# Extra TensorE products of constants in the gated-linear units of two merged mixers

## The reference, cut to what matters

```python
def hybrid_mixer(h, hc, w_in, ret_decay, gate_up, gate_b, gla_norm_g, row_pos, col_pos, need_ctx):
    lat = project_in(h, w_in)
    cx = project_in(hc, w_in)
    ...
    r_lat, r_ctx = bidirectional_scan(retention_inputs(lat, True), retention_inputs(cx, False))
    g_lat, g_ctx = bidirectional_scan(gla_inputs(lat), gla_inputs(cx))

    def merge(r, g, parts):
        ret = from_heads(head_layernorm(r)) * jax.nn.silu(parts[3])
        gla = from_heads(rmsnorm(g, gla_norm_g)) * jax.nn.silu(parts[7])
        return jnp.concatenate([ret, gla], axis=-1)

    y_lat = merge(r_lat, g_lat, lat)
    y_ctx = merge(r_ctx, g_ctx, cx) if need_ctx else None
    return y_lat, y_ctx

def bidirectional_scan(lat_in, ctx_in):
    ...
    c_f, s_f = chunked_gated_linear_attention(cq, ck, cv, ca_f, zero, False)
    x_f, _ = chunked_gated_linear_attention(q, k, v, a_f, s_f, False)
    c_b, s_b = chunked_gated_linear_attention(flip(cq), flip(ck), flip(cv), flip(ca_b), zero, True)
    x_b, _ = chunked_gated_linear_attention(flip(q), flip(k), flip(v), flip(a_b), s_b, True)
    return x_f + flip(x_b), c_f + flip(c_b)
```

## Time and profile before

| | us |
|---|---|
| median of 3 runs | 3764.69 |
| lowest and highest | 3761.97, 3764.97 |
| the profiled execution: its time | 3770.36 |
| the profiled execution: its span | 3768.6 |
| mean granted clock in the span | 0.948 |
| PE busy | 3556.4 (94%) |
| PEld busy | 2815.4 (75%) |
| DVE busy | 1995.8 (53%) |
| ACT busy | 1233.1 (33%) |
| POOL busy | 306.8 (8%) |

### The profile page before, as it was taken

How to read it: one execution, slowest core, us unless ns; L and a number is a source line. 1 busy time by engine, 2 the same in 40 slices (tenths; PEclk the granted TensorE clock), 3 DMA queues, 4 the chain that set the end, 5 groups by cost and what they waited for, 6 DMA issues and landing times.

```text
span 3768.6 us, 42324 instructions
## 1 busy us (share of the span) xinstructions
PE 3556.4 (94%) x17456; PEld 2815.4 (75%) x17456; DVE 1995.8 (53%) x3677; ACT 1233.1 (33%) x2057; POOL 306.8 (8%) x366
## 2 busy tenths in 40 slices
PE   7999999999989999998999989999998998889998
PEld 6656777777867677777986557888887885558886
DVE  5565578857554578854126664323335235654344
ACT  5353432234353433233112222423233212234332
POOL 0200022111130021110000001000001000000000
PEclk9999999999899999999998759999999998779999
DMA  5302245522112245423210001211212310112321
GB/s 165 113 12 78 79 157 168 168 79 95 64 36 79 76 145 171 161 97 124 88 60 20 22 33 50 68 63 61 68 56 76 118 58 27 40 45 90 101 90 67
DMA packets 214109, 317.01 MB, mean 84 GB/s; under 512 B 5304, under 2 KB 162618, under 8 KB 212636
## 3 DMA queue, kind: packets, MB, share of 16 engines
q1 hardware_dynamic: 198108, 243.00, 20.0%
q0 software_dynamic: 15808, 71.31, 5.6%
HBM read 300.66 MB, written 14.49 MB: 84 GB/s over the span
## 4 chain that ended last, share of the span: by engine, by line
PE 80%; DVE 12%; ACT 4%; issue 2%; POOL 1%; DMA 1%; SPq 0%; DVEq 0%; ACTq 0%; POOLq 0%
PE ps L94 78%; DVE t L115 7%; ACT t L100 4%; DVE t L107 3%; POOL t L107 1%; PE ps L97 1%; DVE t L111 1%; DVE t L112 0%; POOL t L134 0%; DVE ps L115 0%; DVE t L121 0%; DMA t<-gates_away 0%; DVE ps L107 0%; DVE t L118 0%; DVE t L125 0%
## 5 line engine op out<-in xcount | busy, mean ns | idle before, releaser
L94 PE MATMUL ps<-t,t 128*128 128x512 f32 (+6 forms) x17040 | 3500.2, 369 | 185.3 <-DVE t L107 89.5
L94 PEld LDWEIGHTS ps<-t,t 128*128 128x128 f32 (+3 forms) x17040 | 2764.2, 192 | 894.7 <-issue 190.5
L100 ACT ACTIVATE t<-t 128x512 f32<-128x512 f32 (+4 forms) x1134 | 806.8, 746 | 1105.1 <-PE ps L94 662.9
L107 DVE TENSOR_TENSOR t<-t,t 128x1024 fp32r<-128x1024 f32 (+5 forms) x850 | 759.2, 919 | 725.3 <-ACT t L100 709.6
L100 ACT ACTIVATE t<-ps 128x512 f32<-128x512 f32 (+5 forms) x506 | 260.5, 537 | 1046.1 <-PE ps L94 995.4
L115 DVE SCALAR_TENSOR_TENSOR t<-t,t,t 128x256 f32<-128x256 f32 (+3 forms) x927 | 437.7, 534 | 14.1 <-ACT t L100 7.4
L107 POOL TENSOR_TENSOR t<-t,t 128x64 f32<-128x64 f32 (+2 forms) x260 | 222.7, 881 | 1778.5 <-ACT t L100 1730.3
L107 DVE TENSOR_TENSOR t<-ps,t 128x512 f32<-128x512 f32 (+4 forms) x293 | 188.1, 660 | 238.2 <-PE ps L94 171.2
L115 DVE SCALAR_TENSOR_TENSOR t<-ps,t,t 128x512 f32<-128x512 f32 (+1 forms) x228 | 139.8, 662 | 281.3 <-PE ps L94 261.2
L118 DVE COPY t<-ps 128x256 f32<-128x256 f32 (+3 forms) x162 | 73.0, 479 | 279.6 <-PE ps L94 261.2
L100 ACT ACTIVATE t<-t,t 128x512 fp32r<-128x512 f32 (+3 forms) x160 | 96.1, 603 | 199.9 <-DVE t L107 127.0
(11 more groups left out here) (33 smaller groups left out, 296.1 us busy)
## 6 DMA issues: line engine op xcount, KB each, us to landing
t<-in_w_ff SPq DMA_DIRECT2D x64, 1024.0 KB, 7.5
t<-in_w_mlp SPq DMA_DIRECT2D x64, 1024.0 KB, 5.5
t<-in_ada_w POOLq DMA_DIRECT2D x48, 1024.0 KB, 5.8
t<-in_w_in SPq DMA_DIRECT2D x30, 1024.0 KB, 5.3
t<-in_w_qkv_o SPq DMA_DIRECT2D x12, 1024.0 KB, 5.2
t<-in_w_mem_kv SPq DMA_DIRECT2D x8, 1024.0 KB, 6.9
t<-in_w_mem_q SPq DMA_DIRECT2D x8, 1024.0 KB, 5.0
t<-in_w_mem_o SPq DMA_DIRECT2D x8, 1024.0 KB, 5.1
```

What stands on the lines that cost most here:

```text
L94: return Issued(self, self.e and self.e.matmul(o, l, r, start=start, stop=stop, skip_group_check=True))
L100: return Issued(self, self.e and self.e.activation(o, i, f, **kw))
L107: return Issued(self, self.e and self.e.tensor_tensor(o, a, b, op))
```

## The change

A work unit gets 12 more products at y = 0, else 6 when no retention task stood between it and the work unit before, else 2. Each multiplies the identity with columns 0 to 255 of the constants (f32, 256 columns) and goes to columns 256 to 511 of `ob`, which nothing reads. They are issued after the wait for the bank and before the wait for gmask. The whole diff:

```diff
--- before.py
+++ after.py
@@ -1157,6 +1157,8 @@
                 if y + 1 < len(work):
                     inside(d, y + 1)
                 opening(ob)
+                for _ in range(idle[0]):
+                    pe.matmul(P[ob][:, 256:512], cst("ident"), CST[:, 0:256], True, True)
                 pe.wait_ge("gmask", l, d, i, par)
                 for j in range(2):
                     h = 2 * j + par
@@ -1179,8 +1181,15 @@
                     "sumsq", ("gla", l), x)
                 free[bk] = [("mean", ("gla", l, x))]
 
+
+        idle, alone = [0], False
         key_scores(0)
         for mixer, u in mixed_units(l):
+            if u[0] == "task":
+                alone = False
+            if u[0] == "work":
+                idle[0] = 12 if u[2] == 0 else 6 if alone else 2
+                alone = True
             (ret if mixer == "ret" else gla)(u)
 
 
```

## The result

The changed kernel takes 3775.84 us (median of 6 runs, 3773.93 to 3791.14), the kernel before in the same session 3763.33 (6 runs). The ratio is 1.0042, 95% interval 1.0027 to 1.0058: slower by 0.42%, 12.5 us. The forecast was 3777, slower by 0.3%. The profiled execution of after took 3773.93 us with a span of 3772.1.

What follows compares the result with a forecast made beforehand. TensorE bounds the kernel (80% of the chain), with some 201 us at half clock in four stretches. Terms +1.2 - 2 + 6 + 6.7 = +11.9 us on the 3764.69 us median gave 3777 us, slower by 0.3%; range 3756 to 3789.

Steps and rivals of the forecast that it cites:

- A: Layer 0, scan direction 0, first inside product to score product 25: 42 added products, forecast +1.2 us.
- D: Layer 1, scan direction 1, first inside product to output projection: 50 added products, twelve delayed by a late bank; forecast +6.7 us.
- B: Layer 0, scan direction 1, first inside product to output projection: 66 added products, DVE sets the end; forecast -2 us.
- C: Layer 1, scan direction 0, up to direction 1's first mean product: 26 added products; forecast +6 us.
- Price of a product: One added f32 product of 256 columns on TensorE: 0.43 us at full clock, 0.85 at half.
- the three waits of rows 4: Layer 0, direction 0: TensorE waits three times 1.38 us for the bank-emptying COPY; clock falls again at some, +4.7 us.
- between: Layer 0, from score product 25 to the first inside product of direction 1; the forecast sum had no term for it.
- the next 23.76 us: Layer 1, direction 1: a var product and five work units at half clock, forecast to become 26.5 us, +2.8.
- Rival 1: Faster by 8 to 10 us, 3756: bank free when TensorE arrives in D, twelve products fill its 5.42 us idle; chance 0.20.
- Rival 2: Clock falls back at the pairs of two products, about 80 us of half clock stay: +25 us, 3790; chance 0.12.
- Rival 3: All four stretches: the clock does not answer to the products at all, near 3888 us; chance 0.04.
- Rival 4: Costs and gains cancel because D's DMA has slack: within 3 us of before, 3765; chance 0.08.

## Why the prediction was right, and where it was not

**Sign and size.** Forecast +11.9 us by the sum, measured +11.9 by the stretches and +12.5 by the medians. That close a sum is luck in part: A and the piece behind it were 6.6 us too high, D 3.4 too low, B 2.3 too low and C 0.8 too low, and A and C move by 4 us or more with nothing changed in them. What is not luck is that the products cost more than the clock gave, and D's late bank.

**Price of a product: right.** 0.43 us at full clock. In the run with the free bank twelve of them ran from 3267.14 to 3272.62, 0.46 each with the last one's way through the array; and a work unit's own twelve records took 1.97 us at full clock, where I had written 2.0.

**A, forecast +1.2, measured -3.6; the piece behind it -1.8, not in the sum.** The failed step is the one that reads "the three waits of rows 4 stay, and the clock will fall at some of them again: I take 10 us left at half clock, +4.7". The waits stayed, the clock didn't fall. Three of them in TensorE's timeline of after:

```profile
2103.47 1.13 PE L94 MATMUL ps<-t 128*128 128x256 f32 x4 [1.38 <-DVE t L118]
2110.82 1.13 PE L94 MATMUL ps<-t 128*128 128x256 f32 x4 [1.42 <-DVE t L118]
2118.56 1.13 PE L94 MATMUL ps<-t 128*128 128x256 f32 x4 [1.38 <-DVE t L118]
```

Each is followed by two products in 1.13 us, full clock. Only 3.4 us of A were left at half clock. At 0.47 those are 1.6 us in place of the 4.7, which brings the forecast to -1.9; the other 1.7 us are within what A moves by itself. And "between", 3.7 us at half clock in before, I had left out though the change could warm it.

**B, forecast -2, measured +0.3: right within its spread.** Full clock and 66 products cancel, and VectorE sets the end, as forecast. The window of the last 12.8 us of B in after:

```profile
2233.90:2246.70 12.80, 1.19 (x2) 0.51 (x3) 12.14 (x27) 9.09 (x23) 0.53 (x1) 0.50 0.00 1
```

TensorE has two records there and VectorE is busy 12.14 us, so the half clock in that piece costs B nothing.

**C, forecast +6, measured +6.8: the steps were right, the figure is not a constant.** The first work unit is late by 4.4 us (forecast 4.3), the second gate bank by 1.2 (1.2), TensorE's wait there grew from 1.95 to 3.02 us and brought the half clock back, and units 2 to 6 added 5.3 (4.8). But C took 79.3 us in another kernel with the same code there, and 61.2 or 65.2 to 65.4 without any product, so my 3 us of spread was too small and the closeness is luck.

**D, forecast +6.7, measured +10.1: the mechanism right, one term mis-sized.** The bank came free late (4.53 us of idle), the work unit started 7.0 us later (6.6), gates_away was issued 4.5 us later (3.9) and took 10.12 us (10.20). The failed step is that the next 23.76 us become 13.1 at full clock, plus 12.9 for 30 products and 0.5 for waits: I took the clock as held through them. TensorE was idle in front of them, waiting for the DMA, and the first 10.2 us ran at 0.50 with six of the products in it; from the var product to the first sum it was +6.7 us (30.44 against 23.76), not +2.8. Behind it the tail was 0.9 us shorter, which the sum did not have: TensorE's first two records in it took 1.15 us there, at full clock, and 2.06 in before.

**The rivals.** Rival 1 (a free bank in D) named the right condition: with the bank free D is 6.9 us shorter, but not level with before. Rival 2 (the clock falls back at the twos) did not come in the changed kernel, but it is refuted in A alone: with a twelve and twos A had no half clock at all, while D, behind the wait for gates_away, stayed at 0.50 for 40.9 us. Rival 3 (the clock does not answer to the products) is refuted: half-clock time fell from 51 to 3.4 us in A, from 83 to 20 in B with its tail, from 24 to 10 in C and from 60 to 30 in D with its tail. Its premise, no idle at all at half clock, holds for the 43.0 us of the earlier trace rows and not for B's whole 75.0, where TensorE was busy 69.58. Rival 4 did not come.

The Trainium skill, "TensorE: Matmul & The Clock Gate", section "Why this matters for your kernels", asks for no long idle gaps between bursts of matmuls, for these bring the clock down. Idle is not the whole of it here: TensorE stayed at 0.50 while busy for 54.58 of 54.60 us, and products put between busy units did change the grant. The same page (section "What's actually happening") says that how many slow products one sees varies from run to run with the clock gate's phase at the kernel's start, that the slow start costs under 1% of a typical kernel's span, and that one should not fit to a count. The 68.0 and 79.3 us of the same code of C in two kernels fit that: they differ by 11.3 us, 0.3% of the span. But a change worth 0.4% cannot be judged while this is left out.

## What to carry to other kernels

Work that only keeps TensorE's clock up is paid in full wherever TensorE is the bound, so find the least that holds the clock (here, in layer 0, two products a unit in place of six and twelve: 22 us instead of 5) and put larger pieces only where TensorE waits anyway, into a bank that is already free. Behind a wait for another engine that stays, such work buys little, and a little of it can be worse than more or none (D in layer 1: 80.7 us with twos, 77.7 with sixes, 67.6 with none); shorten the wait first. No run here has added products of another width, so whether their 256 columns or only their number holds the clock is open. Judge such a change by the same stretch in several kernels, not by one execution's time: a stretch whose code is the same can differ by more than the whole effect.

## What the runs showed that I had not expected

- The same instructions of C, with starts within 0.02 us of each other, took 68.0 and 79.3 us, since the half clock behind the same 3.0 us wait lasted 6.8 us in one and 30.7 us in the other. Without any product in it, C took 61.2 us in four traces (before among them) and 65.2 to 65.4 in five, and one kernel is in both groups.
- With two products a unit TensorE stayed at half clock for 54.60 us of which it was busy 54.58, in layer 1; in layer 0 the same two products kept it at 0.94 over A. What makes the difference is not settled. Both of C's bad cases (79.3 and 85.8 us) begin with the fall at the round trip, but so do the 68.0 us of after, where the clock came back after 6.8 us.
- Waits of 1.4 us left the clock up once there were wide products around them (three in A, 1.38 to 1.42 us), where in before the pieces around waits of 1.38 us ran at half clock in part.
- A kernel with products in A alone gained 5.3 us there and in the piece behind it, and lost them again in B and C, where nothing had changed (+1.2 and +4.1 us): its median is that of before.
